# A ring of weight slots, filled from the model's own weight arrays or from blocks that the host has laid out in order of use

## The reference, cut to what matters

```python
for layer in range(DEPTH):                       # first model, DEPTH = 2
    mod = cond @ ada_w[layer] + ada_b[layer]     # 1024 x 6144
    ...
    mix = even_mixer(h, ...) or gla_mixer(h, ...)
    x = x + gt_m[:, None, :] * mix
    x = x + gt_f[:, None, :] * hier_moe(h, ..., exp_w1[layer], exp_w3[layer], exp_w2[layer])
...
def expert_block(args):                          # 32 experts per layer, top 2 per token
    xi, e = args
    hid = jax.nn.silu(xi @ w1[e]) * (xi @ w3[e]) # w1, w3: 1024 x 512 each
    return hid @ w2[e]                           # w2: 512 x 1024
...
for l in range(DEPTH):                           # second model
    mix = _token_mixer(x, ...)                   # w_in 1024 x N_IN, w_branch, w_o
    x = _layernorm(alpha * x + mix, ...)
    ffn = _hier_moe(x, ...)                      # 32 experts, w_gate and w_up 1024 x 256, w_down 256 x 1024
    x = _layernorm(alpha * x + ffn, ...)
```

## Time and profile before

| | |
|---|---|
| time, median of 3 runs | 2899.12 us (2893.81 to 2905.8) |
| span of the profiled execution | 2894.3 us |
| the same execution's own time | the page gives none beside the span; the three runs lie 0.5 us below to 11.5 us above the span |
| PE busy | 2683.4 us, 93% |
| PE weight loads busy | 1683.4 us, 58% |
| DVE, ACT busy | 642.8 us, 495.5 us |
| mean granted TensorE clock | 0.964 |
| moved by the SP queue | 768.18 MB, 453,872 packets |

### The profile page before, as it was taken

The page is one execution under the profiler, slowest core; times in us unless marked ns, Lnnn a source line. Parts: engine busy times, 40 slices in busy tenths (PEclk is TensorE's granted clock), DMA queues, the critical chain, the costliest instruction groups (busy, mean ns, idle before and its releaser), DMA issues.

```text
span 2894.3 us, 31970 instructions
## 1 busy us (share of the span) xinstructions
PE 2683.4 (93%) x13512; PEld 1683.4 (58%) x13512; DVE 642.8 (22%) x1263; ACT 495.5 (17%) x850; POOL 0.2 (0%) x4
## 2 busy tenths in 40 slices
PE   7987999999998999999999998999999998999997
PEld 5756654444445684444444777865555777865554
DVE  2254330000002231010000533131111433131112
ACT  2321120111012121111110232021111242021111
POOL 0000000000000000000000000000000000000000
PEclk8998999999999999999999999999999899999999
DMA  9474559999998237999999543259998342359992
GB/s 364 147 273 163 204 198 395 393 393 395 394 393 308 88 117 287 396 394 393 394 396 394 177 131 88 86 193 355 342 341 283 90 138 63 133 196 348 341 345 102
DMA packets 454242, 769.65 MB, mean 266 GB/s; under 512 B 12560, under 2 KB 219280, under 8 KB 454032
## 3 DMA queue, kind: packets, MB, share of 16 engines
q1 hardware_dynamic: 453872, 768.18, 74.7%
q10 hardware_dynamic: 288, 0.26, 0.0%
HBM read 767.36 MB, written 1.05 MB: 265 GB/s over the span
## 4 chain that ended last, share of the span: by engine, by line
PE 69%; DMA 18%; DVE 7%; SPq 4%; ACT 2%; issue 1%; DVEq 0%; ACTq 0%
DMA slab<-in_exp_w 17%; PE psum L458 15%; PE psum L490 12%; PE psum L1740 10%; PE psum L1747 8%; PE psum L1771 6%; PE psum L1728 5%; PE psum L634 4%; SPq L413 4%; PE psum L559 1%; PE psum L526 1%; PE psum L1130 1%; PE psum L566 1%; PE psum L525 1%; PE psum L1777 0%
## 5 line engine op out<-in xcount | busy, mean ns | idle before, releaser
L458 PE MATMUL psum<-slab 128*128 (+7 forms) x3400 | 574.1, 327 | 9.1 <-ACT slab L2106 7.1
L458 PEld LDWEIGHTS psum<-slab 128*128 128x128 f32 (+2 forms) x3400 | 480.7, 193 | 138.1 <-issue 95.0
L1740 PE MATMUL psum<-slab 128*64 128x512 f32 x2048 | 473.0, 617 | 61.1 <-DMA slab<-in_exp_w 55.6
L1740 PEld LDWEIGHTS psum<-slab 128*64 128x64 f32 x2048 | 150.2, 141 | 362.4 <-issue 322.5
L490 PE MATMUL psum<-slab 128*128 128x256 f32 x1504 | 338.3, 388 | 19.9 <-ACT slab L550 10.3
L1771 PE MATMUL psum<-slab 128*64 128x512 f32 x1536 | 343.7, 596 | 3.0 <-ACT slab L1795 3.0
L490 PEld LDWEIGHTS psum<-slab 128*128 128x128 f32 x1504 | 292.4, 195 | 65.0 <-issue 16.3
L1728 PE MATMUL psum<-slab 128*128 128x256 f32 x1024 | 232.0, 380 | 3.0 <-DVE slab L1815 3.0
L1747 PE MATMUL psum<-slab 128*64 128x512 f32 x1024 | 226.8, 595 | 0.1
L1771 PEld LDWEIGHTS psum<-slab 128*64 128x64 f32 x1536 | 104.6, 137 | 206.5 <-issue 202.6
L1728 PEld LDWEIGHTS psum<-slab 128*128 128x128 f32 x1024 | 189.5, 190 | 27.1 <-DVE slab L1815 4.0
(11 more groups left out here) (381 smaller groups left out, 1679.7 us busy)
## 6 DMA issues: line engine op xcount, KB each, us to landing
slab<-in_exp_w SPq DMA_DIRECT2D x192, 2048.0 KB, 18.2
slab<-in_w_exp_gate SPq DMA_DIRECT2D x64, 1024.0 KB, 9.3
slab<-in_w_exp_up SPq DMA_DIRECT2D x64, 1024.0 KB, 11.2
slab<-in_w_exp_down SPq DMA_DIRECT2D x64, 1024.0 KB, 8.4
slab<-in_ada_w SPq DMA_DIRECT2D x24, 2048.0 KB, 8.6
slab<-in_w_in SPq DMA_DIRECT2D x64, 512.0 KB, 6.4
slab<-in_even_w_in SPq DMA_DIRECT2D x7, 2048.0 KB, 14.7
slab<-in_gla_w_in SPq DMA_DIRECT2D x6, 2048.0 KB, 14.6
```

The source lines that it names most:

```text
L458: ins = mm(out_ap, lhs, rhs, start=(n == 0), stop=(n == len(pairs) - 1), skip_group_check=True)
L1740: ins = mm(psum[CAP * e:CAP * e + CAP, n, :], xg[:, k, CAP * e:CAP * e + CAP], sl(w[e], KD)[:, k, :], start=(k == 0), stop=(k == KD - 1), ...
```

## The change

The host lays the weights out in the order of use. For the dense stages one array `dense` holds one block of 128 x 4096 floats per fill; for the expert stages `experts1` and `experts2` hold, for each layer and pass, six such blocks. In a block the 16 KB of a partition lie together, and the partitions follow each other. Every fill is then one DMA of 128 contiguous rows. Narrow fills (332, 420 or 16 columns) are packed without gaps, `narrow`, so they too are one run per partition, and only the used columns are moved. `xT` and the output are laid out in the same way (8 KB and 4 KB per partition and transfer). The amounts, the ring, its order and the conditions under which a slot is refilled are the same. Each slot now counts 16 per fill in place of 16 per DMA. The overflow path reads from the new arrays and is written out per expert of a pass.

```diff
-        def fill_cols(w, c0, n, extra=()):
-            def f(s):
-                r = [(sl(s, KD, 0, n), kxn(w, c0, n))]
...
-            def up(w, e):
-                return lambda s: [(sl(s, KD), a[w][l, e].rearrange("(k p) n -> p k n", p=P))]
...
-            def gate_up(e):
-                def f(s):
-                    return [(sl(s, KD, 256 * j, 256), a[w][l, e].rearrange("(k p) n -> p k n", p=P))
-                            for j, w in enumerate(("w_exp_gate_2", "w_exp_up_2"))]
...
+        def narrow(s, n):
+            return ring[:, s, 0:KD * n].rearrange("p (k n) -> p k n", k=KD)
+        wd, we1, we2 = a["dense"], a["experts1"], a["experts2"]
+        def dense_fills(name, first=0, last=None):
+            at, widths = dense_at[name]
+            return [(wd[at + j], widths[j]) for j in range(first, len(widths) if last is None else last)]
...
+        def moe_fills(w):
+            return lambda l, i: [(w[l, i, j], SLOT) for j in range(NR)]
...
-            sp.dma_start(xT, a["xT"].rearrange("(k p) n -> p k n", p=P)).then_inc(sems["inputs_in"], 16)
+            sp.dma_start(xT.rearrange("p k n -> p (k n)"), a["xT"]).then_inc(sems["inputs_in"], 16)
...
-                for dst, src in f(s):
-                    sp.dma_start(dst, src).then_inc(sems[f"slot{s}"], 16)
+                src, n = f
+                sp.dma_start(ring[:, s, 0:n], src[:, 0:n]).then_inc(sems[f"slot{s}"], 16)
...
-                        for dst, src in f(s):
-                            sp.dma_start(dst, src).then_inc(sems[f"slot{s}"], 16)
+                        sp.dma_start(ring[:, s, :], f[0]).then_inc(sems[f"slot{s}"], 16)
...
-        def slot(q, dmas=1):
+        def slot(q):
...
-            q.e.wait_ge(sems[f"slot{s}"], q.due(f"slot{s}", 16 * dmas))
+            q.e.wait_ge(sems[f"slot{s}"], q.due(f"slot{s}", 16))
...
+def columns(w, *parts):
+    c = np.concatenate([np.asarray(w)[:, c0:c0 + n] for c0, n in parts], 1)
+    return c.reshape(KD, P, c.shape[1]).transpose(1, 0, 2).reshape(P, -1)
...
+    e1 = np.stack([up(np.asarray(a[n])).reshape(2, E // 2, 2, P, SLOT) for n in ("exp_w1", "exp_w3")]
+                  + [down(np.asarray(a["exp_w2"])).reshape(2, E // 2, 2, P, SLOT)], 2)
...
+    arrays["dense"] = np.stack(dense)
+    arrays["experts1"], arrays["experts2"] = expert_blocks(inputs)
```

More of the change, by code:

```diff
@@ L214, with build @@
 """.split()
-def build(nc, a, vec_at, vec_w, out):
+def build(nc, a, vec_at, vec_w, dense_at, out):
     ctx = ExitStack()
@@ L306, in out_fills @@
[L306 to L314, removed]
@@ L785, in pe_even_in @@
                 ins = accumulate(psum[CH * half:CH * half + CH, b, 0:S],
-                                 [(sl(s, KD)[:, k, 256:320], hT[:, k, :]) for k in range(KD)])
+                                 [(narrow(s, 332)[:, k, 256:320], hT[:, k, :]) for k in range(KD)])
             ins.then_inc(sems["unit_done"], 1)
@@ L1743, in pe_pair @@
             else:
-                w = [slot(q, 2), slot(q, 2)]
+                w = [slot(q), slot(q)]
                 for k in range(KD):
@@ L1765, in pe_pair @@
                 q.e.wait_ge(sems["xg_ready"], q.due("xg_ready", 2))
-            down = [slot(q), slot(q)] if kind == 1 else [slot(q, 2)] * 2
+            down = [slot(q), slot(q)] if kind == 1 else [slot(q)] * 2
             for half in range(2):
@@ L1825, in pe_experts @@
             n = PAIRS[kind]
-            per = {f"slot{(q.slot + j) % NR}": 16 * kind for j in range(NR)}
+            per = {f"slot{(q.slot + j) % NR}": 16 for j in range(NR)}
             per.update(gatedT_ready=n, results_ready=2 * n, hid_ready=n, hidT_ready=n, xg_ready=2 * n, gated_ready=n)
@@ L2349, in pe_merge @@
             q.e.wait_ge(sems["branch_read"], q.due("branch_read"))
-            late = [slot(q, 4), slot(q, 4)]
-            br = [slot(q, 2), slot(q, 2)]
+            late = [slot(q), slot(q)]
+            br = [slot(q), slot(q)]
             for half in range(2):
@@ L2356, in pe_merge @@
                     for j in range(4):
-                        s = late[j] if j < 2 else slot(q, 4)
+                        s = late[j] if j < 2 else slot(q)
                         for n in range(2):
@@ new lines, in columns, with rows_of, halves, dense_blocks @@
+def columns(w, *parts):
+    c = np.concatenate([np.asarray(w)[:, c0:c0 + n] for c0, n in parts], 1)
+    return c.reshape(KD, P, c.shape[1]).transpose(1, 0, 2).reshape(P, -1)
+def rows_of(w):
+    w = np.asarray(w)
+    return w.reshape(-1, P, w.shape[-1]).transpose(1, 0, 2).reshape(P, -1)
+def halves(w, c0=0, n=D):
+    return [columns(w, (c0 + 512 * j, 512)) for j in range(n // 512)]
+def dense_blocks(a):
+    even, gla = a["even_w_in"][0], a["gla_w_in"][0]
+    blocks = {f"ada{l}": halves(a["ada_w"][l], 0, 6 * D) for l in range(2)}
+    blocks["even_in"] = [columns(even, (QA, 512)), columns(even, (KA, 512)), columns(even, (VA, 512)),
+                         columns(even, (QI, 324), (BA, 8)), columns(even, (QB, 512)), columns(even, (KB, 512)),
+                         columns(even, (VB, 512)), columns(even, (ZA, 512))]
+    blocks["even_out"] = halves(a["even_w_out"][0])
+    blocks["gla_in"] = [columns(gla, (3072, 16))] + halves(gla, 0, 3072)
+    blocks["gla_out"] = halves(a["gla_w_out"][0])
+    for l in range(2):
+        w = a["w_in_2"][l]
+        gate = [columns(w, *[(MIX2["gate"] + n * D + dc * P, P) for n in range(4)]) for dc in range(KD)]
+        latent = np.concatenate([rows_of(a["mla_w_uq_2"][l]), rows_of(a["mla_w_ukv_2"][l])], 1)
+        branch = [np.concatenate([rows_of(a["w_branch_2"][l, 2 * j + i]) for i in range(2)], 1) for j in range(2)]
+        blocks[f"mix2_{l}"] = [columns(w, (MIX2["conv"], 512)), columns(w, (0, 416), (MIX2["ff"], 4)),
+                               columns(w, (MIX2["sbq"], 512)), columns(w, (MIX2["sbv"], 256), (MIX2["fxv"], 256)),
+                               latent, columns(w, (MIX2["fxq"], 512))] \
+            + gate[:6] + branch + gate[6:] + halves(a["w_o_2"][l])
+    return blocks
@@ new lines, in expert_blocks @@
+def expert_blocks(a):
+    up = lambda w: w.reshape(2, E, KD, P, -1).transpose(0, 1, 3, 2, 4)
+    down = lambda w: w.reshape(2, E, -1, P, D).transpose(0, 1, 3, 2, 4)
+    e1 = np.stack([up(np.asarray(a[n])).reshape(2, E // 2, 2, P, SLOT) for n in ("exp_w1", "exp_w3")]
+                  + [down(np.asarray(a["exp_w2"])).reshape(2, E // 2, 2, P, SLOT)], 2)
+    both = np.concatenate([up(np.asarray(a[n])) for n in ("w_exp_gate_2", "w_exp_up_2")], -1)
+    both = both.reshape(2, E // 4, 2, 2, P, SLOT)
+    two = down(np.asarray(a["w_exp_down_2"])).reshape(2, E // 2, 2, P, 2 * D).transpose(0, 1, 3, 2, 4)
+    e2 = np.concatenate([both, two.reshape(2, E // 4, 2, 1, P, SLOT)], 3)
+    return np.ascontiguousarray(e1.reshape(2, E // 2, NR, P, SLOT)), np.ascontiguousarray(e2.reshape(2, E // 4, NR, P, SLOT))
```

129 lines of the change are left out of this document (49 added, 80 removed).

## The result

The changed kernel took 2812.21 us, median of four runs (2811.83 to 2816.43), against 2896.53 us of the kernel before, whose four runs now include one more. The ratio is 0.971 (95% interval 0.9691 to 0.9729). The forecast was 2819 us in a range of 2807 to 2862.

The account below looks back on a forecast made before the run. Transfers were taken to bound only the kind 1 expert stages; 2 x (38.3 + 1.7) = 80 us off the 2894.3 us span gave 2814.3, and 4.8 us from span to median made 2819 us, range 2807 to 2862.

Parts of the forecast that it names:

- What bounds the kernel: Kind 1 expert stages are bounded by the transfer rate, by 2.9 us per pass; kind 2 is an even demand.
- The price of a packet: Weight transfers: 9.5 ns per packet plus 4.811 us of bytes per slot; 16 KB runs give 4.887 us, 429 GB/s.
- rival 2: Kind 1 transfers: the rate stops at 4 KB's 410 GB/s; gain 37 us, 2862 us; chance 0.18.
- Rivals 2 and 3: Weight transfers: rate stops at 410 GB/s, 2862 us, chance 0.18; or no gain beyond 512 B, 2899 us, chance 0.05.
- The sum of kind 1: Both kind 1 stages: 38.3 us from 88 faster slots plus 1.7 us from faster last matmuls per layer, 80 us.
- What is late next: Kind 1: PE allows 40.5 us per layer, so transfers still end last, by some 2 us in a whole stage.
- Rival 1: Kind 1: PE becomes the bound, gaining 40.5 and 40.6 us plus 1.7 each; 84.5 us, 2815 us; chance 0.22.
- The start: Kernel start: faster `xT` against later positions landing, between -0.5 and +3 us; taken as 0.
- Before 400 us nothing moves by over 3 us: Expected sign in the profile after: all before 400 us stays within 3 us of its old time.
- The positions' landing: At the start, positions could land up to 6 us later than 4.8 us, 3 us of it covered until 9.54.
- The other parts: Kind 2, dense stages, SP's issue, LDWEIGHTS and instruction fetches: each taken as 0 gain.
- Rival 4: Kind 1 transfers: power-of-two address distances lower the rate; slower, 3032 us at 344 GB/s; chance 0.05.

Follow-up runs that it names:

- kind 1 only: The kernel before, with the new 16 KB blocks for the kind 1 expert stages alone: 2812.5 us, ratio 0.9709.
- half `w2`: The changed kernel, with kind 1's `w2` fills moving only the first 8 KB per partition from the second pass on: 2812.6 us, ratio 0.97.
- all but kind 1: The changed kernel, with kind 1 filled from the model's old arrays in 2 and 4 KB runs: 2901.8 us, ratio 1.0011.
- the second profile: The changed kernel run and profiled once more, with no edit: 2816.6 us, ratio 0.9722.

## Why the prediction was right, step by step

**What bounds the kernel.** Right: the two kind 1 stages were bound by transfers and no other stage was; "kind 1 only" has all of the gain.

**The price of a packet.** Right in mechanism and size: 9.5 ns and 4.811 us, 429 GB/s foretold and 428 to 429 measured. The constants' row at 409 GB/s with a share of 0.96 misled towards rival 2; its edges were in it. Rivals 2 and 3 are out.

**The sum of kind 1.** 80 us foretold, 79.8 measured: 38.2 twice by the stream (38.3 foretold), 1.7 twice by the last matmuls at full clock.

**What is late next.** Partly right. I wrote that the transfers end last "by some 2 us in a whole stage" and expected passes of 29.1 to 29.4 us. A pass of PE is 28.93 us, not 29.03, and the slack is used up after six passes; the last eight follow the transfers at 29.36. The half `w2` puts what the transfers still cost at 3.4 us in the first layer and 3.6 in the second. Rival 1, PE as the bound, has the nearer time (2815) and named the slack, but not the mechanism of the whole stage: with less to move the late passes go from 29.36 to 28.93 us, so it is the transfers that they follow. Here two cases 4 us apart couldn't be told by the total.

**The start.** The step was open between -0.5 and +3 us, and taken as 0. DVE's first work waits for `xT` until 9.14 us in place of 9.54:

```profile
9.14 0.43 DVE L683 CAST slab<-slab 128x512 f32<-128x512 int32 x1 [9.14 <-DMA slab<-in_xT]
```

so the transfers gave 0.4 us. The rest of the 5.1 us by which kind 1 begins earlier is the clock's: it is there with the old fills ("kind 1 only", 393.75) and missing with the new ("all but kind 1", 398.82, and the second profile, 399.16). "Before 400 us nothing moves by over 3 us" thus failed in the first profile, by something that the prediction had no term for. The positions' landing, 5.3 us in place of 4.8, stayed covered.

**The other parts.** Kind 2 kept its pace, PE 240.00 of 240 us:

```profile
1875.00:2115.00 240.00, 240.00 (x1308) 133.36 (x1307) 33.59 (x81) 31.80 (x58) 0.00 (x0) 1.00 0.89 342
```

I expected a DMA share of 0.8, from the rates; it is 0.89. The same reckoning, 34.3 us of transfers in 36.8, gives 0.93 for before, where the row reads 1.01: the share read 0.08 to 0.09 over it both times, and I should have seen that in the first. It cost nothing.

SP is no longer held by its queue. Timeline of SP's queue, before and after; six fills take 3.85 us where the first four alone took 14.81:

```profile
1.81 14.81 SPq L394 DMA_DIRECT2D slab<-in_ada_w  x4
```

```profile
1.79 3.85 SPq L337 DMA_DIRECT2D slab<-in_dense  x6
```

With that "us to landing" changes its meaning: the constants take 39.8 us from issue in place of 21.8, and land at 45.5 us in place of 49.1, since they were issued at 5.68 and not at 27.34.

**The size in all.** 2819 against 2812.2. Kind 1 is exact; the difference is the start, 5.1 us, a loss of 1.2 later, and the offset from span to median, where I added 4.8 us and 1.6 (2812.2 - 2810.6) was due. In every run here the time is 1.6 to 1.7 us above its own span; by that the profiled run of before took some 2896 us (an estimate), 3 under the median of three that I went by. How far under 2819 the time fell is in part the clock's doing: the second set of runs of the same kernel has 2816.6.

**Rival 4.** The slower side didn't come: the new blocks are contiguous, and even at 2 MiB between partitions the rate is 413 GB/s, over the 388 below which it decides. A way in which such a change does go wrong is another that I hadn't listed: a DMA that covers one half of the partitions, 39% slower than before.

## What to carry to other kernels

Look for a stage whose DMA rate stands still while the matmul engine waits once per pass, and fit the price of a packet from two lengths in the same trace: it was constant from 1 to 32 KB here, so the rate that longer runs bring can be computed before anything is built. Then compute what is late next, per pass and over the stage, since that caps the gain; where a stage is an even demand under its ceiling, as kind 2 is here, longer runs bring nothing. Keep all 128 partitions in each DMA, or a set spread over both halves, as the even ones are; and judge an edit worth a few us by the passes of its stage, not by the time.

## What the runs showed of the hardware

- A packet costs a DMA engine 9.5 ns beside its bytes, on this one core: 348, 387, 410, 422, 428 to 429 and 432 GB/s at 1, 2, 4, 8, 16 and 32 KB.
- A DMA of partitions 0 to 63 or 64 to 127 runs at 213 GB/s, of the 64 even or odd ones at 429.
- 16 KB runs that are 2 MiB apart go at 413 GB/s, side by side at 428.
- Outside the stages that an edit touches, the granted clock of TensorE differs between profiles of one kernel. At 1.2 GHz 16 matmuls took 3.64 us in place of 1.92, and kind 1 began at 399.16 or 393.83 us. Runs of the changed kernel spread over 12 us (2811.8 to 2824.3) and those of before, at granted clocks of 0.968 to 0.960, over 19 (2886.8 to 2905.7).
